# Memory values one pair later in a bank of their own, and V turned by VectorE's squares and by the load of its chunks

## What is computed

```python
proj = x @ w_in                                   # q, k, v, gate of the attention; pool; LRU; q, gate of the memory part; merge gates
# stick-breaking attention, per head, query block i, key blocks n <= i
z = einsum('bhqd,bhnkd->bhqnk', q_blk, k_pre) * scale
w = where(valid, exp(log_sigmoid(z) + within + later), 0)
o = einsum('bhqnk,bhnkd->bhqd', w, v_pre)
# memory cross attention, per head
scores = einsum('bshd,bmhd->bhsm', qh, k) / sqrt(128)
out = einsum('bhsm,bmhd->bshd', softmax(scores), v)
# then: * silu(gate), @ w_branch, * sigmoid(merge), sum, @ w_out, residual, layer norm
```

## Time and profile before

| | us |
|---|---|
| median of 3 runs (lowest, highest) | 2305.55 (2305.26, 2305.99) |
| the profiled execution, its own time | 2303.36 |
| span of the profiled execution | 2301.6 |
| TensorE busy in it | 2283.5 |
| VectorE busy | 1441.2 |
| ScalarE busy | 1060.4 |
| GpSimd busy | 1224.2 |

### The profile page before, as it was taken

How to read it: one execution, slowest core, us unless ns; L and a number is a source line. 1 busy time by engine, 2 the same in 40 slices (tenths; PEclk the granted TensorE clock), 3 DMA queues, 4 the chain that set the end, 5 groups by cost and what they waited for, 6 DMA issues and landing times.

```text
span 2301.6 us, 29983 instructions
## 1 busy us (share of the span) xinstructions
PE 2283.5 (99%) x10824; PEld 1887.2 (82%) x10824; DVE 1441.2 (63%) x1658; ACT 1060.4 (46%) x1627; POOL 1224.2 (53%) x847
## 2 busy tenths in 40 slices
PE   9999999999999999999999999999999999999998
PEld 6888888888878888888888888888888778878887
DVE  7555552763486477468877777723844595486476
ACT  5555542342484255332576676632342683355220
POOL 1666653864456355435476566644763556345341
PEclk9999999999999999999999999999999999999999
DMA  6544422124343344373344544322133334354442
GB/s 234 188 158 156 145 75 96 55 83 133 108 112 124 133 126 141 109 278 143 107 159 139 166 154 130 118 95 75 55 123 135 85 99 146 128 144 126 145 166 83
DMA packets 114419, 297.84 MB, mean 129 GB/s; under 512 B 11232, under 2 KB 41056, under 8 KB 113248
## 3 DMA queue, kind: packets, MB, share of 16 engines
q1 hardware_dynamic: 112544, 290.68, 38.1%
q10 hardware_dynamic: 1728, 5.24, 0.7%
HBM read 216.19 MB, written 71.30 MB: 125 GB/s over the span
## 4 chain that ended last, share of the span: by engine, by line
PE 96%; issue 2%; DVE 2%; DMA 1%; ACT 0%; DVEq 0%; ACTq 0%
PE J L817 20%; PE J L819 20%; PE J L818 20%; PE AO L989 8%; PE ZZ L989 8%; PE AO L817 2%; PE AO L819 2%; PE AO L818 2%; PE ZZ L819 2%; PE ZZ L818 2%; PE ZZ L817 2%; PE AO L943 1%; PE JX L943 1%; PE ZZ L1024 1%; PE ZZ L912 1%
## 5 line engine op out<-in xcount | busy, mean ns | idle before, releaser
L2326 POOL TENSOR_TENSOR WLS<-SR,WHS 128x512 fp32r<-128x512 f32 x264 | 411.5, 1577 | 109.4 <-ACT WHS L1151 101.6
L817 PE MATMUL J<-XBH,WHS 128*128 128x512 f32 x1152 | 452.3, 393 | 0.0
L819 PE MATMUL J<-XBH,WLS 128*128 128x512 f32 x1152 | 449.1, 390 | 0.0
L818 PE MATMUL J<-XBL,WHS 128*128 128x512 f32 x1152 | 448.8, 390 | 0.0
L817 PE MATMUL J<-XBH,WH 128*128 128x512 f32 x864 | 340.0, 394 | 0.2
L819 PE MATMUL J<-XBH,WL 128*128 128x512 f32 x864 | 337.0, 390 | 0.0
L818 PE MATMUL J<-XBL,WH 128*128 128x512 f32 x864 | 336.7, 390 | 0.0
L2318 POOL TENSOR_TENSOR SR<-RAW 128x512 f32<-128x512 f32 x71 | 106.4, 1498 | 293.0 <-DMA RAW<-w 254.5
L819 PEld LDWEIGHTS J<-XBH,WLS 128*128 128x128 f32 x1152 | 216.3, 188 | 46.0
L817 PEld LDWEIGHTS J<-XBH,WHS 128*128 128x128 f32 x1152 | 216.4, 188 | 43.6 <-DVE XBL L1703 0.2
L818 PEld LDWEIGHTS J<-XBL,WHS 128*128 128x128 f32 x1152 | 216.4, 188 | 43.5 <-issue 0.2
(11 more groups left out here) (298 smaller groups left out, 4751.2 us busy)
## 6 DMA issues: line engine op xcount, KB each, us to landing
RAW<-w SPq DMA_DIRECT2D x144, 512.0 KB, 3.7
pk_m<-MB SPq DMA_DIRECT2D x56, 512.0 KB, 5.1
MB<-pk_m SPq DMA_DIRECT2D x48, 512.0 KB, 4.1
KC<-pk_k SPq DMA_DIRECT2D x40, 512.0 KB, 5.3
VC<-pk_v SPq DMA_DIRECT2D x40, 512.0 KB, 4.4
BRAW<-w SPq DMA_DIRECT2D x64, 256.0 KB, 5.1
XRAW<-xt SPq DMA_DIRECT2D x8, 1024.0 KB, 13.2
pk_v<-STL SPq DMA_DIRECT2D x16, 512.0 KB, 5.0
```

The costliest lines, as they stand in the source:

```text
L817: nc.tensor.matmul(to, wh, xh, start=first, stop=True, skip_group_check=True)
L818: nc.tensor.matmul(to, wh, xl, start=False, stop=True, skip_group_check=True)
L819: return nc.tensor.matmul(to, wl, xh, start=False, stop=True, skip_group_check=True)
L2326: low = G_.tensor_tensor(WLS[:, k, :], SR[:, k, :], WHS[:, k, :].bitcast(F32), ALU.subtract)
```

## The change

Two edits are made together.

**Memory values.** TensorE's `memory_values` of head h moves from behind pair XA0 + h + 1 into the pair after that: chunk 0 ahead of piece 1, chunk 1 ahead of piece 5. Both chunks go to the bank JX one after the other (the last head's chunk 1 to ACC). The scores of head h stand directly behind their pair, and their wait for `y_f` is gone; `memory_values` has it instead. VectorE makes XQL ahead of the split of the weights, and multiplies the outputs in hooks 2 and 4 of the later pair. SyncE loads the values of the memory in hook 6.

**V.** TensorE's transposes of V, and its two waits for them, are gone. VectorE turns V in its 32 by 32 squares (two transposes of 128x512, SBUF to SBUF, written with a step of four elements), ScalarE copies all 1024 columns at once, VectorE subtracts all 1024 at once from SBUF. `pk_v` has another layout, so that the load of a chunk puts the squares in place: four DMAs of 32 partitions in runs of 128 elements instead of one DMA of 128 partitions in runs of 1024. `VC` becomes `[2, P, BLOCKS]`, so that the weights that TensorE loads for a product with V are 128 columns with a step of four elements.

```diff
-        VC = at("VC", R + 68.0625, [BLOCKS, 2, P], F32R)
+        VC = at("VC", R + 68.0625, [2, P, BLOCKS], F32R)
...
-        pk_v = nc.dram_tensor("pk_v", (HEADS, P, SEQ // P, 2, P), F32).ap()
+        pk_v = nc.dram_tensor("pk_v", (HEADS, 2, P, SEQ // P, P), F32).ap()
...
-                    sp.dma_start(pk_v[h, :, half * TB:(half + 1) * TB, part, :],
+                    sp.wait_ge(v_blk, hh + 1)
+                    sp.dma_start(pk_v[h, part, :, half * TB:(half + 1) * TB],
...
                 wait_if(sp, pv_done, 2 * n)
-                sp.dma_start(VC[:].bitcast(F32), pk_v[h, :, BLOCKS * (k ^ 1):BLOCKS * (k ^ 1) + BLOCKS]).then_inc(v_in, 16)
+                for q in range(GROUPS):
+                    rows = pk_v[h, :, :, GROUPS * (k ^ 1) + q].rearrange("s (i x) m -> x (s i) m", i=GROUPS)
+                    to = VC[SQUARE * q:SQUARE * (q + 1)].bitcast(F32).rearrange("x s (i r) b -> x (s i) (r b)", i=GROUPS)
+                    sp.dma_start(to, rows).then_inc(v_in, 16)
...
-                if l < 2 * HEADS and l % 2 and i in (10, 12):
-                    turn(g, 0 if i == 10 else 1)
...
-                    mm = pass3(OB[:, j * P + q:j * P + HALF], (VC[:, BLOCKS - 1 - b, 0, :], VC[:, BLOCKS - 1 - b, 1, :]),
+                    mm = pass3(OB[:, j * P + q:j * P + HALF], (VC[:, 0, :, BLOCKS - 1 - b], VC[:, 1, :, BLOCKS - 1 - b]),
...
-                    if c:
-                        wait_if(pe, y_f, y_count(half, 3, h))
...
-            def memory_values(half, h):
+            def memory_values(half, h, chunks):
                 hh = half * HEADS + h
                 pe.wait_ge(vm_back, 32 * (hh + 1))
-                for c in range(NC):
+                for c in chunks:
                     pe.wait_ge(pt_done, NC * hh + c + 1)
+                    if h or c:
+                        pe.wait_ge(y_f, y_count(half, 3, h) + (c if h + 1 < HEADS else 0))
                     for m in range(MEM // P):
-                        mm = pass3(BR[1][c][:], (VM[0][:, m, :], VM[1][:, m, :]), (PTH[c][:, m, :], PTL[c][:, m, :]), m == 0)
+                        mm = pass3(values_bank(h, c)[:], (VM[0][:, m, :], VM[1][:, m, :]), (PTH[c][:, m, :], PTL[c][:, m, :]), m == 0)
...
+                def earlier_values(h):
+
+                    return {1: lambda: memory_values(half, h, (0,)), 5: lambda: memory_values(half, h, (1,))}
+
                 for h in range(HEADS):
-                    pair(g0 + XA0 + h)
-                    if h:
-                        memory_values(half, h - 1)
+                    pair(g0 + XA0 + h, earlier_values(h - 2) if h > 1 else {})
                     memory_scores(half, h)
-                merge(half, 3, {13: lambda: memory_values(half, HEADS - 1)})
+                hooks = earlier_values(HEADS - 2)
+                hooks[13] = lambda: memory_values(half, HEADS - 1, range(NC))
+                merge(half, 3, hooks)
...
-                nc.scalar.copy(places(g // PAIRS, STL)[2][:, part * C:(part + 1) * C], J[(g + 1) % 2][:]).then_inc(v_hi, 1)
+                act.wait_ge(v_tr, NC * (hh + 1))
+                nc.scalar.copy(places(g // PAIRS, STL)[2][:], places(g // PAIRS, ST)[1][:]).then_inc(v_hi, 1)
...
+            def turn_values(g):
...
+                for c in range(NC):
+                    t = slice(c * C, (c + 1) * C)
+                    V_.transpose(to[:, t].rearrange("p (q x b) -> p b q x", q=GROUPS, b=BLOCKS),
+                                 v[:, t].rearrange("p (b n) -> p b n", b=BLOCKS)).then_inc(v_tr, 1)
...
+            def rest_values(g):
...
+                V_.tensor_tensor(lo[:], places(g // PAIRS, ST)[1][:], hi[:].bitcast(F32), ALU.subtract).then_inc(v_blk, 1)
```

More of the change, by code:

```diff
@@ L417, in by_tile, with values_bank @@
             return keys.rearrange("p (b g r) -> p b g r", g=GROUPS, b=MEM // P)
+        def values_bank(h, c):
+            return ACC if c and h + 1 == HEADS else JX
         def as_moved(c):
@@ L492, in keep_values @@
                 for part, of in ((1, places(half, STL)[1]), (0, places(half, STL)[2])):
-                    sp.wait_ge(v_blk, 2 * hh + 2)
-                    sp.dma_start(pk_v[h, :, half * TB:(half + 1) * TB, part, :],
+                    sp.wait_ge(v_blk, hh + 1)
+                    sp.dma_start(pk_v[h, part, :, half * TB:(half + 1) * TB],
                                  of[:].bitcast(F32).rearrange("p (b m) -> p b m", m=P)).then_inc(v_kept[part], 16)
@@ L667, in merge @@
                         hooks[3] = lambda: move_blocks(half, HEADS - 1)
+                        hooks[6] = lambda: load_memory_values(half, HEADS - 1)
                     if n == 2:
@@ L773, in _ @@
                         elif n == 2:
-                            hooks = {0: lambda: load_memory_keys(half, h), 3: lambda: move_blocks(half, h - 1),
-                                     13: lambda: load_memory_values(half, h)}
+                            hooks = {0: lambda: load_memory_keys(half, h), 3: lambda: move_blocks(half, h - 1)}
+                            if h > 1:
+                                hooks[6] = lambda: load_memory_values(half, h - 1)
                         pair(g0 + first + h, hooks)
@@ L842, in piece @@
                     wait_if(pe, ad_done, 4 * (g - 1) + 2)
-                    if 2 <= l <= 2 * HEADS and l % 2 == 0:
-                        pe.wait_ge(v_blk, 2 * (half * HEADS + l // 2))
                     if l == 0 and half:
@@ L952, in values @@
                 pe.wait_ge(wt_lo, 2 * (gp + 1))
-                pe.wait_ge(v_in, 16 * (n + 1))
+                pe.wait_ge(v_in, 16 * GROUPS * (n + 1))
                 blocks = j + 2 if diag else BLOCKS
@@ L1259, in piece, with values_hi @@
                     shared(g, 1, 0, 0, 6)
-                if g % PAIRS < 2 * HEADS and g % 2 and i in (10, 12):
-                    values_hi(g, 0 if i == 10 else 1)
-            def values_hi(g, part):
+                if g % PAIRS < 2 * HEADS and g % 2 and i == 10:
+                    values_hi(g)
+            def values_hi(g):
                 hh = g // PAIRS * HEADS + g % PAIRS // 2
-                act.wait_ge(v_tr, 2 * hh + part + 1)
-                nc.scalar.copy(places(g // PAIRS, STL)[2][:, part * C:(part + 1) * C], J[(g + 1) % 2][:]).then_inc(v_hi, 1)
+                act.wait_ge(v_tr, NC * (hh + 1))
+                nc.scalar.copy(places(g // PAIRS, STL)[2][:], places(g // PAIRS, ST)[1][:]).then_inc(v_hi, 1)
             def split_keys(g):
@@ L1736, in summed @@
                 V_.tensor_tensor(d, bank[:], d, ALU.add).then_inc(ad_done, 1)
-            def turned(g, part):
+            def turn_values(g):
                 hh = g // PAIRS * HEADS + g % PAIRS // 2
-                t = slice(part * C, (part + 1) * C)
-                dve.wait_ge(v_hi, 2 * hh + part + 1)
+                dve.wait_ge(ad_done, 4 * g + 2)
                 dve.wait_ge(k_kept, 32 * (hh + 1))
-                hi, lo = places(g // PAIRS, STL)[2], places(g // PAIRS, STL)[1]
-                V_.tensor_tensor(lo[:, t], J[(g + 1) % 2][:], hi[:, t].bitcast(F32),
-                                 ALU.subtract).then_inc(v_blk, 1)
+                _, to, v = places(g // PAIRS, ST)
+                for c in range(NC):
[3 more added lines that the diff above has]
+            def rest_values(g):
+                hh = g // PAIRS * HEADS + g % PAIRS // 2
+                dve.wait_ge(v_hi, hh + 1)
+                _, lo, hi = places(g // PAIRS, STL)
+                V_.tensor_tensor(lo[:], places(g // PAIRS, ST)[1][:], hi[:].bitcast(F32), ALU.subtract).then_inc(v_blk, 1)
             def rest_of_first(g, parts=(0, 1)):
@@ L1790, in piece @@
                     rest_of_sums(g + 1, False)
-                if l < 2 * HEADS and l % 2 and i in (10, 12):
-                    turned(g, 0 if i == 10 else 1)
+                if l < 2 * HEADS and l % 2 and i == 10:
+                    turn_values(g)
+                if l < 2 * HEADS and l % 2 and i == 12:
+                    rest_values(g)
             def pair(g, after={}, first=0):
@@ L2131, in memory_turned, with memory_output @@
                                      ).then_inc(pt_done, 1)
-            def memory_output(half, h):
+            def memory_output(half, h, chunks):
                 hh = half * HEADS + h
-                for c in range(NC):
+                for c in chunks:
                     dve.wait_ge(xo_done, NC * hh + c + 1)
@@ L2138, in memory_output @@
                     y = Y[h][:, c * C:(c + 1) * C].rearrange("p (t i q) -> p i t q", i=GROUPS, q=SQUARE)
-                    made = BR[1][c].rearrange("p (i t q) -> p i t q", i=GROUPS, q=SQUARE)
+                    made = values_bank(h, c)[:].rearrange("p (i t q) -> p i t q", i=GROUPS, q=SQUARE)
                     V_.tensor_tensor(y, made, y, ALU.mult).then_inc(y_f, 1)
@@ L2240, in hooks_of @@
                 def hooks_of(h):
-                    return {1: lambda: memory_max(half, h), 3: lambda: memory_norm(half, h),
```

(14 more changed lines are left out.)

## The result

The changed kernel takes 2383.4 us in the median of four runs (2381.3 to 2385.5), the kernel before 2305.4 us beside it: a ratio of 1.034 with a 95% interval of 1.032 to 1.036. It is 78 us slower. The forecast of 2292.6 us (2285 to 2304) had the wrong sign, and its second rival, "Slower, by the step of the weights", gave 2388 us.

A forecast was written before the change was run, and what follows sets the result against it. The prediction took TensorE, busy for 2283.5 of 2301.6 us, to bound the kernel. Its terms, -7.0 - 8.9 + 2.0 + 1.0 = -12.9 us, took 2305.5 to 2292.6 us, range 2285 to 2304.

The forecast's parts named there:

- second rival: Products with V paced by a slower weight load: doubled, 95 us, 2388 us; half of it 2340; chance 0.17.
- What bounds the kernel: TensorE is busy for 2283.5 of 2301.6 us, so only its work and its waits can move the end.
- transposes removed: TensorE's 64 transposes of V go, 16 groups at 0.44 us each: 7.0 us gained.
- Memory values moved: Two TensorE waits behind pairs XA0 + 1 to XA0 + 3 end, 1.49 us at six places: 8.9 us gained.
- three other waits: TensorE waits that could come instead: scores for XQL, values for PTL, next pair for its sums; nothing taken.
- the bound that was given: Later softmax at piece 13 of the merge, where the last head's values stand: at most 0.6 us a half.
- The weights with a step: TensorE's 864 weight loads for products with V, columns 16 bytes apart: nothing or 95 us lost; nothing taken.
- V on the other engines: VectorE gets 1.1 to 3.4 us more a head; TensorE's waits at heads' ends in half 1: 2.0 us lost.
- slow bound: Each VectorE transpose of V takes 1.25 us if the written step of four elements halves the rate, otherwise 0.62.
- The load of V's chunk: Four issues instead of one, landing in 4.3 to 4.9 us: 1 us lost, between nothing and 3.
- the first rival: V's load decides, through half of the ports: waiting 7 to 26 us, time 2298 to 2317; chance 0.12.
- The sum: All terms together: -7.0 - 8.9 + 2.0 + 1.0 = -12.9 us, from 2305.5 to 2292.6 us.

The follow-up runs named there:

- step 2: Kernel before, only the weights of the products with V read two elements (8 bytes) apart: 2307.8 us, ratio 1.001.
- steps of two and three: Kernel before, only the weights of the products with V read two or three elements apart: 2307.8 us and 2352.2 us.
- one-load kernel: Changed kernel with contiguous weights for the products with V, and one 512 KB issue for a chunk instead of four: 2292.1 us, ratio 0.995.
- version that regroups at the write: Changed kernel with V turned in natural order and regrouped where written to DRAM, contiguous weights, four loads in 1024-byte runs: 2297.2 us, ratio 0.996.
- contiguous-weights kernel: Changed kernel, only the products with V read 128 contiguous columns as weights, without the step; four loads kept: 2296.5 us, ratio 0.996.

## Why the prediction was wrong

**What bounds the kernel, and transposes removed**: held. TensorE's work sets the end before and after. No run took out the transposes alone; in the trace of before the distances from each of the 64 to the next start sum to 6.3 us, and the product behind ten of the 16 groups is followed 0.09 us late, another 0.9: together 7.2.

**Memory values moved**: held, 8.9 us forecast, 9.2 between the profiled spans and 11.4 between the medians. None of the three other waits that were weighed came in the kernel with this part alone. In the changed kernel one came, 0.6 us for PTL at the last head of half 1, the bound that was given.

**The weights with a step**: this step failed, and by it the sign. The two bounds enclosed it (nothing, or 95 us), and right was the observation that any real slowing of the weight load is fully seen: only the few ns by which a stream of 256 columns (0.12 us) is longer than the weight load (0.11 us) cover some of it. Wrong was the choice between them. It read "if a step of 16 bytes halves the best rate of reading, 1.1 a ns is left" (by its own numbers already a little under the 1.2 at which the weights are read): it counted columns. The 2.2 columns a ns of contiguous streaming are four to a piece, so 0.55 pieces a ns; with each column in a piece of its own a quarter is left, 0.55 columns a ns, and the load takes 128 / 0.55 = 0.23 us. Both numbers for this stood in the prediction: 512 columns in 0.23 us, and the lines of 16 bytes of the Trainium skill, SBUF — State Buffer, section "Door 1: The DMA port swizzle". The measured 0.235 us is what they give. That section of the Trainium skill says that two hits on a line hide the access. The runs bear this out for the weights (step 2 costs 2 us over 864 products), but not for the streamed operand, where two columns to a line take 227 ns instead of 118. Its other statement, that 4-byte elements may be four apart for free, they contradict (93 us). The access to a line was weighed as a vague penalty where it could have been turned into a price. That the rival's doubling, 95 us, lay so near was luck: no working stood behind it, and steps of two and three cost 2 and 46 us.

**V on the other engines**: the size was a little off. The two transposes take 1.09 us each, nearer to the slow bound of 1.25 than to 0.62, and the subtraction 1.22. That is 2.0 us more a head in the place of 1.1 to 3.4. TensorE's waits for it (scans, WTL and QL, in the one-load kernel) are 3.4 us in the place of 2.0, at the heads' ends of half 1, as forecast: 1.2, 0.5, 0.5 and 1.2 us, where 1.1 stood for the first head and 0.3 for each of the others.

**The load of V's chunk**: mis-sized. Forecast 1 us, 3 as the bound; with contiguous weights the wait is 3.5 us, and one issue instead of four is worth 2.7 us of waiting and 4.4 us of time. At a load of 6.0 us the prediction's terms leave no gain at all, not 2 us, once VectorE's 2.0 are counted. A doubling by the half of the ports, the first rival, is not seen: 4.6 us in the median against 4.4 for the one load of before. What was not counted is that behind another transfer the four stretch further than one does (7.5 us at 1171 against 5.1). The number of issues and the shorter runs were changed together there; four loads with runs twice as long, in the version that regroups at the write, still wait 3.8 us. In the changed kernel half of the wait is hidden, 1.7 us instead of 3.5, and the step costs less there than alone (86.9 against 92.9 us). That the slower products give each load a longer window would explain both, but was not tested.

**The sum**, then: with the step at the 93 us measured for it alone, 2305.5 - 7.0 - 8.9 + 2.0 + 1.0 + 93 = 2385.6 us, against 2383.4 measured. The other errors nearly cancel, which is luck: the memory part gave 11.4 us for 8.9, the rest of V's part lost some 2 where a gain of 4.0 stood, and the step cost 86.9 in this company. Only one term carried the forecast to the wrong side, and its rival had been given 0.17.

## What to carry to other kernels

Count the 16-byte pieces that an operand of TensorE touches in each partition, and not only its columns: in these runs some 1.8 ns each, if that is more than the time that its columns need anyway. For the 4-byte data of this kernel that leaves room for a step of two in the weights and none in a stream of 256 columns. A saving on the fullest engine (7 us of transposes) must be set against every instruction that then reads what the new layout holds: here 64 instructions went, and 864 then read their weights with a step. And where a price has only bounds, and they lie on both sides of the sign, work the bound out from the rate of the nearest row before choosing by feel.

## What the runs showed of the hardware that was not expected

- TensorE's reading of 4-byte columns from SBUF goes by 16-byte pieces on both sides at nearly the same rate, and both run at once: a stream of 128 pieces in 227 ns, a weight load of 128 pieces every 235 ns, while 256 columns (64 pieces) are streamed beside it. One after the other, 192 pieces at 1.8 ns would take 0.35 us.
- VectorE's transposes of 128x512 pay for a written step of four elements: 1.09 us with the regrouping of the changed kernel against 0.68 in natural order. The tile rows of the contiguous-weights kernel and of the version that regroups at the write:

```profile
L1746 DVE STREAM_TRANSPOSE ST<-ST x16: 1059/1088/1114, 69.7 to 1394.0; 128x512 f32<-128x512 f32 x16
```

```profile
L1744 DVE STREAM_TRANSPOSE ST<-ST x16: 661/685/703, 69.7 to 1394.4; 128x512 f32<-128x512 f32 x16
```

- A 128 KB write to DRAM in runs of 128 bytes lands in 3.3 us in the median, and the first head's eight (1 MB) are through 8.9 us behind the first issue. The eighth is issued 5.4 us behind the first, so most of this is the issuing. The same bytes in two writes take 6.9 us in the kernel before (runs of 512 bytes) and 4.6 in the contiguous-weights kernel (runs of 4096 bytes): short runs do cost, but far less here than feared. The page's row of the version that regroups at the write:

```profile
pk_v<-STL SPq DMA_DIRECT2D x64, 128.0 KB, 3.3
```
